# A two-block transformer kernel: filter loads and products of the start, the turning of attention probabilities, gate row, tokens and tail

## Chip, cores and metric

The kernel runs on one core of one Trainium2 chip. Everything is float32. The metric is the device time of one execution in microseconds (us), the median of several runs.

## What is computed

One token sequence of 256 x 1024 goes through two blocks. Cut to what matters:

```python
# first block: modulation from c, then attention and a gated feed-forward network
mod = silu(c) @ w_ada + b_ada                      # 1024 -> 6 x 1024
hn = rms_norm(h, norm1_g) * (1 + scale1) + shift1
qa, ka, va, qb, kb, vb = split(hn @ w_in)          # 1024 -> 3072
o_a = dilated_window_attention(...)                # 8 heads, three windows merged: counts * exp(s)
p = softmax(q1 k1 + bias) - lam * softmax(q2 k2 + bias); o_b = p @ v   # 4 heads
h = h + gate1 * ([o_a, o_b] @ w_out)
h = h + gate2 * ((silu(gate) * val) @ w_down)      # 1024 -> 5632, conv, 2816 -> 1024
# second block: long convolution (Hyena) beside a gated linear recurrence, then experts
z = sin(fr1 * (pos @ w1 + b1)); z = sin(fr2 * (z @ w2 + b2)); filt = (z @ w3) * window
aff = softmax(h @ router_w); gates, idx = top_k(aff.T, 32)   # 16 experts take 32 tokens each
y = (silu(xg @ w1[e]) * (xg @ w3[e])) @ w2[e] * gates        # 1024 -> 2048 -> 1024 per expert
return rmsnorm(x + g2 * scatter(y), final_g)
```

## The kernel before

It is one program with five instruction streams written out by hand, one per engine, that wait for each other on semaphores. `S["name"]` is a semaphore; `done(ins, name)` raises it on VectorE, and `link` makes VectorE wait for its own instruction. The order on an engine is the order in its function. `MM` is a TensorE product; one float32 product is two MATMUL records in the profile, a transpose is one.

Weights come in units of 1 MB, issued by SyncE in the order of `units` into `ring`, which has 8 slots; a slot is refilled when the unit in it is used (`unit_done`). The first eight units are the first third of the modulation weights w_ada. `mod_products(m)` multiplies unit m with the conditioning, in four column groups; `copy_mod_rows(g)` on ScalarE copies the rows of eight such units out, and `mod_columns(g)` turns them with four transposes. `third_layer` multiplies the filter's hidden values (`sint`) with `w3w`, one product for each of eight pieces. VectorE's `window` reads them. `features` are the products of the input projection with `w_in`, a unit of 32 records each. Counts for the windows (`cntW`) come over GpSimd's queue.

The attention goes in 16 pairs p. Pairs 0 to 7 are two heads of the first kind and a block of 128 queries; pairs 8 to 15 (`isb`) are the two maps of one head of the second kind. TensorE's loop over p is: `scores(p + 2)`, a modulation product (p < 6), `turn_probs(p)`, a modulation product (6 <= p < 14), `pv(p - 1)`. VectorE does `pair_max(p)` (bias and maximum, into `sS`), the sum and reciprocal and `diag` (`pair_diag(p)`: the identity scaled by 1/sum), and `pair_out(p)`. ScalarE does the exponentials of p (into `sE`) and then the copy of the turned probabilities of p - 1 (`probs_copied`). `turn_probs` multiplies the probabilities with `diag`, which turns and scales them at once:

```python
if isb:
    last = MM(PTB[...], sE[:, b, i, ...], diag[:, b, i, :], start=(i == 0), stop=(i == 1))
else:
    last = MM(PTB[...], sC[:, b, i, ...], diag[:, b, i, :], start=True, stop=True)
```

In the routing VectorE ranks 16 x 256 affinities in four rounds of `max` and `match_replace`, TensorE meanwhile turns the tokens (`token_major`), and broadcasts the gate row (`gate_rows`), and then it turns the places. An expert then goes through `expert_pick` (32 tokens, products with a one-hot `ohx`), a copy on ScalarE (`xrow`), two transposes (`tokens_turned`), `expert_tokens` on VectorE (gain, then shift, into `xe`), `expert_up` (16 units), `expert_gate_rows`, `expert_down` (8 units) and `expert_scatter`. Expert weights come in pairs of units, 2 MB each, 12 pairs an expert, 192 in all, into eleven places in SBUF (`PAIR`). Pair g is issued when pair g - 11 is used (`expert_unit_done`), so pair 11 waits for the first two units of the first expert. The last pair comes as two units. At the end ScalarE squares the four banks of 128x512, VectorE makes the inverse and multiplies (`final_rows`), and SyncE stores two blocks of 512 KB.

## Time and profile before

| | |
|---|---|
| median of 3 runs | 1646.39 us (1646.09 to 1648.83) |
| the profiled execution | 1647.9 us, its span 1646.1 us |
| TensorE busy | 77% of the span, weight loads 43% |
| VectorE, ScalarE, GpSimd busy | 24%, 13%, 3% |
| chain that ended last | TensorE 48%, DMA 42%, VectorE 4% |
| mean granted TensorE clock | 0.895 |

The span is the time from the first to the last instruction of the profiled execution; its own time is 1.8 us longer. The median of the runs is 1.5 us below that time. PE is TensorE, DVE is VectorE, ACT is ScalarE, POOL is GpSimd, SP is SyncE; PEld are weight loads.

### The profile page before, as it was taken

How to read it: one execution, taken by the hardware profiler on the slowest of the kernel's cores; microseconds unless marked ns; L12 is line 12 of the kernel's file. 1: busy time of each engine (PE TensorE's matmuls, PEld its weight loads, DVE VectorE, ACT ScalarE, POOL GpSimd, SP SyncE). 2: the span in 40 equal slices, each digit the busy share in tenths (PEclk: the TensorE clock that was granted, in tenths of full speed). 3: DMA queues.
4: the chain of work that ended last, by engine and by line, in shares of the span. 5: the costliest groups of instructions: out<-in, count | busy, mean ns of one | idle time of the engine just before them, and what ended most of it. 6: DMA issues, size and time to landing. Idle time of an engine off the chain costs nothing.

```text
span 1646.1 us, 16563 instructions
## 1 busy us (share of the span) xinstructions
PE 1272.1 (77%) x7160; PEld 702.0 (43%) x7160; DVE 394.1 (24%) x800; ACT 217.3 (13%) x423; POOL 51.0 (3%) x75
## 2 busy tenths in 40 slices
PE   5999999999999999988555655665665656666555
PEld 3776678888888878852111111111111111111111
DVE  4577653454032547530000000000000000000001
ACT  2323422122202231120000000000000000000001
...
GB/s 359 205 195 287 322 191 325 214 228 214 199 154 136 176 127 178 205 262 425 428 427 428 428 428 427 427 428 428 428 427 428 428 428 429 427 427 429 428 428 286
DMA packets 109978, 545.04 MB, mean 331 GB/s; under 512 B 5908, under 2 KB 73269, under 8 KB 78997
## 3 DMA queue, kind: packets, MB, share of 16 engines
...
## 4 chain that ended last, share of the span: by engine, by line
PE 48%; DMA 42%; DVE 4%; another core or an unknown queue 3%; ACT 1%; issue 1%; SPq 0%; DVEq 0%
DMA arena<-in_exp_w_dram 29%; PE L L1594 12%; DMA ring<-in_exp_w_dram 9%; PE L L1821 7%; PE X L2029 5%; PE L L1790 4%; DMA tok<-in_exp_w_dram 3%; PE X L1762 3%; PE X L2057 2%; PE L L1940 2%; PE L L1728 2%; DMA ring<-in_w_ada_dram 2%; PE L L2068 1%; PE L L1605 1%; PE X L1870 1%
## 5 line engine op out<-in xcount | busy, mean ns | idle before, releaser
L2029 PE MATMUL X<-arena,HR 128*32 128x512 f32 x1104 | 171.1, 753 | 102.9 <-DMA arena<-in_exp_w_dram 93.0
L1594 PE MATMUL L<-tok,ring 128*128 128x256 f32 x960 | 213.0, 383 | 2.0 <-ACT tok L605 1.6
L1594 PEld LDWEIGHTS L<-tok,ring 128*128 128x128 f32 x960 | 183.7, 192 | 34.8 <-issue 9.8
L2029 PE MATMUL X<-ring,HR 128*32 128x512 f32 x784 | 119.1, 736 | 82.5 <-DMA ring<-in_exp_w_dram 77.5
L2057 PE MATMUL X<-arena,HI 128*32 128x512 f32 x592 | 94.9, 772 | 56.7 <-DMA arena<-in_exp_w_dram 52.6
L1436 DVE TENSOR_TENSOR HR<-HR,X 128x512 f32<-128x512 f32 x16 | 11.0, 688 | 515.6 <-ACT HR L860 515.6
L2029 PEld LDWEIGHTS X<-arena,HR 128*32 128x32 f32 x1104 | 34.3, 125 | 230.0 <-DMA arena<-in_exp_w_dram 153.3
L1821 PE MATMUL L<-tok,ring 128*128 128x256 f32 x448 | 99.4, 379 | 0.0
L2029 PEld LDWEIGHTS X<-ring,HR 128*32 128x32 f32 x784 | 23.6, 120 | 168.8 <-DMA ring<-in_exp_w_dram 120.7
L1821 PEld LDWEIGHTS L<-tok,ring 128*128 128x128 f32 x448 | 84.3, 190 | 13.5 <-issue 2.8
L2057 PE MATMUL X<-ring,HI 128*32 128x512 f32 x320 | 55.3, 826 | 32.8 <-DMA ring<-in_exp_w_dram 30.1
L860 ACT ACTIVATE HR<-X 128x512 f32<-128x512 f32 x16 | 9.6, 597 | 528.1 <-PE X L2029 528.1
L1790 PE MATMUL L<-arena,ring 128*128 128x256 f32 x352 | 77.5, 379 | 0.3 <-DVE arena L1196 0.3
L1441 DVE TENSOR_TENSOR HI<-X,HI 128x512 f32<-128x512 f32 x16 | 11.1, 692 | 277.5 <-PE X L2057 277.5
L1790 PEld LDWEIGHTS L<-arena,ring 128*128 128x128 f32 x352 | 66.7, 190 | 9.7 <-DVE arena L1196 0.7
L2057 PEld LDWEIGHTS X<-arena,HI 128*32 128x32 f32 x592 | 18.7, 127 | 122.2 <-DMA arena<-in_exp_w_dram 82.0
L2068 PE MATMUL L<-HI,HR 64*128 64x512 f32 x128 | 38.9, 730 | 14.5 <-DVE HI L1441 14.5
L858 ACT ACTIVATE HR<-X 128x256 f32<-128x256 f32 x16 | 6.1, 384 | 312.0 <-PE X L2012 312.0
L2029 PE MATMUL X<-tok,HR 128*32 128x512 f32 x160 | 27.8, 831 | 18.4 <-DMA tok<-in_exp_w_dram 17.3
L2057 PEld LDWEIGHTS X<-ring,HI 128*32 128x32 f32 x320 | 10.2, 132 | 72.4 <-DMA ring<-in_exp_w_dram 49.3
L1190 DVE SCALAR_TENSOR_TENSOR arena<-L,cols,arena 128x255 f32<-128x255 f32 x44 | 19.2, 478 | 79.8 <-ACT arena L724 79.8
L549 POOL TENSOR_TENSOR HI<-HI 128x256 f32<-128x256 f32 x16 | 9.9, 617 | 883.4 <-DVE HI L1446 820.5
...
## 6 DMA issues: line engine op xcount, KB each, us to landing
...
ring<-in_w_in_dram SPq DMA_DIRECT2D x34, 1024.0 KB, 5.5
...
ring<-in_w_ada_dram SPq DMA_DIRECT2D x24, 1024.0 KB, 8.8
ring<-in_w_up_dram SPq DMA_DIRECT2D x22, 1024.0 KB, 7.3
arena<-in_ada_w_dram POOLq DMA_DIRECT2D x13, 1024.0 KB, 7.2
ring<-in_ada_w_dram SPq DMA_DIRECT2D x11, 1024.0 KB, 5.0
```

Source lines behind the costliest of these rows:

```text
L1190: last = V.scalar_tensor_tensor(o_[:, 1:T], u_[:, 0:T - 1], colC[:, C_W0 + c:C_W0 + c + 1], o_[:, 1:T], ALU.mult, ALU.add)
L1594: last = MM(L[:, j % 4, m * T:m * T + T], w[:, k, m * P:m * P + P], src(k), start=(k == 0), stop=(k == KT - 1))
L1605: last = MM(L[:, j % 4, t * T:t * T + T], src[:, k, t * P:t * P + P], w[:, k, :], start=(k == 0), stop=(k == KT - 1))
L1728: last = MM(L[:, j % 4, m * T:m * T + T], w[:, k, m * P:m * P + P], oT[:, k, :], start=(k == 0 and m == 0), stop=(k == KT - 1), skip_group ...
L1762: last = MM(bank[:, x * T:x * T + T], wk, hk, start=(k == 0), stop=(k == KT - 1))
L1790: last = MM(L[:, pos["wdn"][m // 2] % 4, (m % 2) * T:(m % 2) * T + T], w[:, kk, m * P:m * P + P], aT[:, 2 * i + kk, :], start=(i == 0 and ...
L1821: last = MM(L[:, j % 4, x * T:x * T + T], wk, hk, start=(k == 0), stop=(k == KT - 1))
L1870: last = MM(o_, uA[(n - 1) % 2][:, h, t * P:t * P + P], crossed(h, t, LEVELS[n - 1]), start=True, stop=True)
L1940: last = MM(L[:, j % 4, m * T:m * T + T], w[:, k, m * P:m * P + P], yTh[:, k, :] if k < HG else yTg[:, k - HG, :], start=(k == 0 and m == ...
L2029: last = MM(X[CAP * j:CAP * j + CAP, w, :], xe[:, k % 2, k // 2, :], mslot(g, u)[:, j * 512:j * 512 + 512], start=(k == 0), stop=(k == KT ...
L2057: last = MM(X[CAP * b:CAP * b + CAP, 2, :], hTe[:, 2 * x + c, CAP * j:CAP * j + CAP], mslot(g, u)[:, c * D + nb * 512:c * D + nb * 512 + 5 ...
L2068: MM(XB[2 * n + t], ge[h0:h0 + HD, t, :], ys[h0:h0 + HD, :], start=False, stop=True, skip_group_check=True).then_inc(S["scatter_done"], 1)
```

## The change

Its name says: mixer order; filter loads in 128 rows with products dealt, and scaled probabilities; gate row and tokens in parts, with turned identities. What it does:

- The three small inputs of the sine layers become one array of 128 x 448, the third filter matrix one of 128 x 1024 (two halves of its columns below each other) in place of 64 x 2048. Both, and the window, are loaded over ScalarE's queue, with the identity first. The counts are loaded later, behind the last unit of the first eight. The second sine layer is computed twice, on partitions 0 to 63 and 64 to 127.
- The four first filter products stand between `mod_products` 4, 5, 6 and 7 (one, two, one). `keep_busy(bank, n)` puts n transposes of the identity, which nobody reads, into a bank: 3 and 8 around `mod_columns(0)`, 4, 7, 2 and 3 in the routing and the first expert, 13, 2 and 4 in the last expert.
- The probabilities are scaled by ScalarE (`probs_scaled`) and then turned by plain transposes. For the second kind of head VectorE first combines the two maps. ScalarE's copy of the turned ones comes one pair later than before.
- The gate row is computed in two halves, after the first and the third ranking round; its copy comes behind the four token copies; the places go to another bank. The token copies go by blocks of tokens. `expert_tokens` works on two halves.
- The last unit lands in two halves; the final squares take two banks at once; the output is stored in four parts of 256 KB.

```diff
+def filter_rows(v, z):
+
+    w1, w2, w3 = (np.asarray(v[f"hy_pos_w{n}_2"], np.float32)[0] for n in (1, 2, 3))
+    sine = np.zeros((P, T + 192), np.float32)
+    sine[0:33, 0:T], sine[0:33, T:T + 64] = z, w1
+    sine[0:64, T + 64:T + 192] = np.concatenate([w2, w2], axis=1)
+    return sine, w3.reshape(64, 2, 2 * C).transpose(1, 0, 2).reshape(P, 2, C)
...
+        zw, w1w, w2w = sinew[0:33, 0:T], sinew[0:33, T:T + 64], sinew[0:64, T + 64:T + 192]
...
-                if n == 2:
-                    sp.dma_start(w3w[0:64, :], a["hy_pos_w3_2"][0]).then_inc(S["filter_landed"], 16)
-                    sp.dma_start(winw[:, :, :], a["k_win"]).then_inc(S["filter_landed"], 16)
...
-                sp.dma_start(mslot(g, 1), w[e, j, :, 2048:4096]).then_inc(S["last_unit_landed"], 16)
+                for c in range(2):
+                    sp.dma_start(mslot(g, 1)[:, c * D:c * D + D], w[e, j, :, 2048 + c * D:2048 + c * D + D]).then_inc(S[f"last_half{c}_landed"], 16)
...
-                sp.wait_ge(S["out_ready"], t + 1)
-                sp.dma_start(out[0, t * P:t * P + P, :], outw[:, t, :]).then_inc(S["out_stored"], 16)
-            sp.wait_ge(S["out_stored"], 16 * TT)
+                for n in range(2):
+                    sp.wait_ge(S["out_ready"], 2 * t + n + 1)
+                    sp.dma_start(out[0, t * P:t * P + P, n * 512:n * 512 + 512], outw[:, t, n * 512:n * 512 + 512]).then_inc(S["out_stored"], 16)
+            sp.wait_ge(S["out_stored"], 32 * TT)
...
             load(dftE[:, :, :, :], a["k_dft"][:, 0:2, :, :], "dftE_landed")
+            load(cntW[:, :], a["k_cnt"], "counts_landed")
...
+            load(sq0[:, :], a["k_sq0"], "sq0_landed")
             load(cols[:, :], a["p_cols"], "cols_landed")
-            load(sq0[:, :], a["k_sq0"], "sq0_landed")
-            for dst, src in ((zw[0:33, :], a["k_z"]), (w1w[0:33, :], a["hy_pos_w1_2"][0]), (w2w[0:64, :], a["hy_pos_w2_2"][0])):
-                load(dst, src, "sine_landed")
+            load(sinew[:, :], a["p_sine"], "sine_landed")
+            load(w3w[:, :, :], a["p_third"], "filter_landed")
+            load(winw[:, :, :], a["k_win"], "filter_landed")
...
-                        act.wait_ge(S["probs_turned"], p - 1)
+                        act.wait_ge(S["inv_ready"], p - 1)
...
+                if 1 <= p <= NP_:
+                    q = p - 1
+                    b = q % 2
+                    act.wait_ge(S["inv_ready"], q + 1)
+                    for i in range(2 if q < 8 else 1):
+                        last = A(sC[:, b, i, :], sC[:, b, i, :], ACT.Copy, scale=rz[:, 2 * b + i:2 * b + i + 1])
+                    last.then_inc(S["probs_scaled"], 1)
                 if p in (6, 15):
                     copy_mod_rows(1 if p == 6 else 2)
-                if p >= 1:
-                    q = p - 1
+                if p >= 2:
+                    q = p - 2
...
-                A(x2[:, n % 2, (n // 2) * 512:(n // 2) * 512 + 512], XB[n], ACT.Copy, scale=rr[:, n % 2:n % 2 + 1]).then_inc(S["lin_emptied_by_act"], 1)
+                A(x2[:, n // 2, (n % 2) * 512:(n % 2) * 512 + 512], XB[n], ACT.Copy, scale=rr[:, n // 2:n // 2 + 1]).then_inc(S["lin_emptied_by_act"], 1)
+            act.wait_ge(S["gate_rows"], 1)
+            A(g2b[:, :], X[:, 2, :], ACT.Copy).then_inc(S["gate_row_ready"], 1)
...
+                act.wait_ge(S["scatter_done"], 4 * NE - 2 + 2 * t)
+                b0 = pos["xnat"][2 * t] % 4
+                A(outw[:, t, :].rearrange("p (n d) -> p n d", n=2), L[:, b0:b0 + 2, :], ACT.Square,
+                  accum_out=fs[:, t:t + 1]).then_inc(S["final_sq"], 1)
...
-                link(V.reciprocal(rz[:, 2 * b:2 * b + 2], zs[:, 2 * b:2 * b + 2]))
+                inv = V.reciprocal(rz[:, 2 * b:2 * b + 2], zs[:, 2 * b:2 * b + 2])
                 if isb:
-                    link(V.tensor_scalar(rz[:, 2 * b + 1:2 * b + 2], rz[:, 2 * b + 1:2 * b + 2], neglam, None, ALU.mult))
-                for i in range(2):
-                    last = V.tensor_scalar(diag[:, b, i, :], ident, rz[:, 2 * b + i:2 * b + i + 1], None, ALU.mult)
-                done(last, "diag_ready")
+                    link(inv)
+                    r1 = rz[:, 2 * b + 1:2 * b + 2]
+                    link(V.scalar_tensor_tensor(r1, r1, neglam, zs[:, 2 * b:2 * b + 1], ALU.mult, ALU.mult))
+                    inv = V.scalar_tensor_tensor(sC[:, b, 0, :], sE[:, b, 1, :], r1, sE[:, b, 0, :], ALU.mult, ALU.add)
+                done(inv, "inv_ready")
...
+                turned = TURNB.rearrange("p (x q c) -> p x q c", x=2, q=4)
+                for x in range(2):
+                    V.tensor_tensor(xe[:, x, :, :], turned[:, x, :, :], gain_of[:, x, :, :], ALU.mult).then_inc(S["expert_scaled"], 1)
+                    dve.wait_ge(S["expert_scaled"], 2 * e + x + 1)
+                    V.tensor_tensor(xe[:, x, :, :], xe[:, x, :, :], shift_of[:, x, :, :], ALU.add).then_inc(S["expert_tokens"], 1)
...
+            def keep_busy(bank, n):
+
+                for _ in range(n):
+                    nc.tensor.transpose(bank[:, 0:P], ident, ident)
...
-            for m in range(1, 4):
+            MM(aux("sin2")[:, 0:T], w2w, sint[0:64, 1, :], start=True, stop=True).then_inc(S["sin2_done"], 1)
+            for m in range(1, 8):
                 mod_products(m)
-            third_layer(0)
-            for m in range(4, 8):
-                mod_products(m)
+                if 4 <= m < 7:
+                    third_layer((0, 1, 3)[m - 4], (1, 2, 1)[m - 4])
+            keep_busy(X[:, 2, :], 3)
             mod_columns(0)
+            keep_busy(X[:, 2, :], 8)
...
-                pe.wait_ge(S["diag_ready"], p + 1)
+                pe.wait_ge(S["probs_scaled"], p + 1)
                 if p >= 1:
                     pe.wait_ge(S["probs_copied"], p)
-                for kt in range(TT):
-                    for i in range(2):
-                        if isb:
-                            last = MM(PTB[:, kt * P:kt * P + P], sE[:, b, i, kt * P:kt * P + P], diag[:, b, i, :], start=(i == 0), stop=(i == 1))
-                        else:
-                            last = MM(PTB[:, (2 * i + kt) * P:(2 * i + kt) * P + P], sC[:, b, i, kt * P:kt * P + P], diag[:, b, i, :], start=True, stop=True)
+                for i in range(1 if isb else 2):
+                    for kt in range(TT):
+                        last = nc.tensor.transpose(PTB[:, (2 * i + kt) * P:(2 * i + kt) * P + P], sC[:, b, i, kt * P:kt * P + P], ident)
                 last.then_inc(S["probs_turned"], 1)
...
-            for k in range(KT):
-                h0 = HD * (k // 4)
-                last = MM(X[h0:h0 + HD, 2, (k % 4) * P:(k % 4) * P + P], ones[:, 0:HD], dg[:, k, :], start=True, stop=True)
+            for part in range(2):
+                pe.wait_ge(S["ranked"], 1 + 2 * part)
+                for k in range(4 * part, 4 * part + 4):
+                    h0 = HD * (k // 4)
+                    last = MM(X[h0:h0 + HD, 2, (k % 4) * P:(k % 4) * P + P], ones[:, 0:HD], dg[:, k, :], start=True, stop=True)
+                keep_busy(X[:, 0, :], (4, 7)[part])
             last.then_inc(S["gate_rows"], 1)
-            pe.wait_ge(S["gate_row_ready"], 1)
             reached(pe, "places")
             for t in range(TT):
-                last = nc.tensor.transpose(X[:, 2, t * NE:t * NE + NE], rs[0:NE, 2, t * P:t * P + P], ident[0:NE, 0:NE])
+                last = nc.tensor.transpose(X[:, 1, t * NE:t * NE + NE], rs[0:NE, 2, t * P:t * P + P], ident[0:NE, 0:NE])
...
+                if e == 0:
+                    keep_busy(X[:, 0, :], 2)
...
+                    if u < 2:
+                        pe.wait_ge(S["expert_tokens"], 2 * e + u + 1)
...
-                    elif g == LASTG:
-                        pe.wait_ge(S["last_unit_landed"], 16)
                     j, x = (u - 16) // 2, (u - 16) % 2
                     for c in range(2):
+                        if g == LASTG and x == 1:
+                            pe.wait_ge(S[f"last_half{c}_landed"], 16)
...
+                    if e == NE - 1:
+                        keep_busy(X[:, 0, :], {19: 13, 21: 2, 23: 4}.get(u, 0))
```

How this stands in the streams: first TensorE at the start. L1540 is `mod_products` (4 products a unit), L1570 `third_layer`, L1561 `mod_columns`, L1594 the first projection unit. Before:

```order
L1616 MATMUL L<-arena 64x256
L1540 MATMUL X<-ring,HI 32x512 x12
L1570 MATMUL L<-arena 128x512 x4
L1540 MATMUL X<-ring,HI 32x512 x16
L1561 MATMUL X<-sq,HI 128x128 x4
L1594 MATMUL L<-tok,ring 128x256 x16
```

And in the change, where L1567 is `mod_products`, L1598 `third_layer`, L1516 `keep_busy`, L1588 `mod_columns` and L1622 the projection:

```order
L1644 MATMUL L<-arena 128x256
L1567 MATMUL X<-ring,HI 32x512 x16
L1598 MATMUL L<-arena 128x512
L1567 MATMUL X<-ring,HI 32x512 x4
L1598 MATMUL L<-arena 128x512 x2
L1567 MATMUL X<-ring,HI 32x512 x4
L1598 MATMUL L<-arena 128x512
L1567 MATMUL X<-ring,HI 32x512 x4
L1516 MATMUL X<-sq 128x128 x3
L1588 MATMUL X<-sq,HI 128x128 x4
L1516 MATMUL X<-sq 128x128 x8
L1622 MATMUL L<-tok,ring 128x256 x16
```

The filter products no longer stand together ahead of four units, but one, two and one between them.

Second, ScalarE in the attention, at the pairs where the first kind of head begins. L685 are exponentials, L695 the copy of turned probabilities. Before:

```order
L685 ACTIVATE arena<-arena,small 128x256 x4
L695 ACTIVATE arena<-L 128x512
L685 ACTIVATE arena<-arena,small 128x256 x2
L695 ACTIVATE arena<-L 128x512
L685 ACTIVATE arena<-arena,small 128x256 x2
```

And in the change, where L698 are exponentials, L705 the scalings and L715 the copy:

```order
L698 ACTIVATE arena<-arena,small 128x256 x4
L705 ACTIVATE arena<-arena,small 128x256 x2
L698 ACTIVATE arena<-arena,small 128x256 x2
L705 ACTIVATE arena<-arena,small 128x256 x2
L715 ACTIVATE arena<-L 128x512
L698 ACTIVATE arena<-arena,small 128x256 x2
L705 ACTIVATE arena<-arena,small 128x256 x2
L715 ACTIVATE arena<-L 128x512
```

The first copy stands behind the exponentials of two more pairs and the scalings of one more pair.

Third, TensorE in the routing. L1974 is `token_major`, L2000 the gate row, L2005 the places, L2012 the first pick, L2017 its transposes and L2029 the first expert's products. Before:

```order
L1974 MATMUL L<-sq,tok 128x128 x4
L2000 MATMUL X<-HI,sq 64x128 x8
L2005 MATMUL X<-sq,rs 128x16 x2
L2012 MATMUL X<-tok,HI 32x256 x8
L2017 MATMUL X<-sq,HR 128x128 x2
L2029 MATMUL X<-arena,HR 32x512 x16
```

And in the change, with L2028 the gate row and L1516 `keep_busy`:

```order
L2000 MATMUL L<-sq,tok 128x128 x4
L2028 MATMUL X<-HI,sq 64x128 x4
L1516 MATMUL X<-sq 128x128 x4
L2028 MATMUL X<-HI,sq 64x128 x4
L1516 MATMUL X<-sq 128x128 x7
L2033 MATMUL X<-sq,rs 128x16 x2
L2040 MATMUL X<-tok,HI 32x256 x8
L1516 MATMUL X<-sq 128x128 x2
L2047 MATMUL X<-sq,HR 128x128 x2
L1516 MATMUL X<-sq 128x128 x3
L2062 MATMUL X<-arena,HR 32x512 x16
```

Eleven transposes now stand between the gate row and the places, and five around the turning of the first tokens.

## Rows read from the trace of the kernel before

**Rows 1.** The page, part 2: GB/s in 40 equal slices of the span.

```profile
GB/s 359 205 195 287 322 191 325 214 228 214 199 154 136 176 127 178 205 262 425 428 427 428 428 428 427 427 428 428 428 427 428 428 428 429 427 427 429 428 428 286
```

**Rows 2.** Timeline, TensorE at the start: start us, us, what, records, idle before.

```profile
33.48 1.46 PE L1540 MATMUL X<-ring,HI 128*32 128x512 f32 x8 [2.32 <-DMA ring<-in_w_ada_dram]
35.64 1.12 PE L1561 MATMUL X<-sq,HI 128*128 128x128 f32 x4 [0.70 <-ACT HI L593]
38.38 10.05 PE L1594 MATMUL L<-tok,ring 128*128 128x256 f32 x32 [1.62 <-ACT tok L605]
...
52.95 7.17 PE L1594 MATMUL L<-tok,ring 128*128 128x256 f32 x32
```

**Rows 3.** Windows: busy by engine, then granted clock, DMA share and GB/s.

```profile
16.00:18.00 2.00, 2.00 (x11) 1.77 (x10) 1.86 (x8) 0.04 (x1) 0.00 (x0) 1.00 0.95 201
...
36.00:37.00 1.00, 0.76 (x4) 0.35 (x2) 0.17 (x1) 0.00 (x0) 0.00 (x0) 0.50 1.11 350
```

**Rows 4.** SyncE's issues from 19.75 us, and the first one's time to landing.

```profile
19.75 34.91 SPq L437 DMA_DIRECT2D ring<-in_w_in_dram  x9
...
ring<-in_w_in_dram SPq DMA_DIRECT2D x1, 1024.0 KB, 16.7
```

**Rows 5.** Timeline: TensorE's transposes, at the kernel's start and at 93 us.

```profile
10.08 3.64 PE L1497 MATMUL L<-sq,arena 128*128 128x128 f32 x16 [10.08 <-DMA sq<-in_k_sq_dram]
...
14.97 3.72 PE L1515 MATMUL X<-tok,sq 128*128 128x256 f32 x16
...
93.24 1.91 PE L1497 MATMUL L<-sq,arena 128*128 128x128 f32 x16
```

**Rows 6.** Timeline, TensorE in the attention: a round of each half.

```profile
165.29 1.06 PE L1540 MATMUL L<-ring,arena 128*32 128x512 f32 x8
...
166.29 1.16 PE L1669 MATMUL L<-arena 128*128 128x128 f32 x8
...
167.38 0.67 PE L1683 MATMUL L<-arena 128*64 128x128 f32 x8
...
167.97 0.70 PE L1656 MATMUL X<-arena 64*128 64x256 f32 x4
...
168.60 1.06 PE L1540 MATMUL L<-ring,arena 128*32 128x512 f32 x8
...
189.10 1.16 PE L1667 MATMUL L<-arena 128*128 128x128 f32 x8
...
192.46 1.16 PE L1667 MATMUL L<-arena 128*128 128x128 f32 x8
```

**Rows 7.** Groups by form from 157 to 206 us: count, busy us, mean ns.

```profile
L1057 DVE CUSTOM_DVE_ANT_0 arena<-X,arena 128x256 f32<-128x256 f32 x28 | 10.8, 422 | 12.7 <-PE X L1656 12.7
...
L682 ACT ACTIVATE arena<-arena,small 128x256 f32<-128x256 f32 x16 | 7.9, 497 | 0.0
...
L695 ACT ACTIVATE arena<-L 128x256 f32<-128x256 f32 x8 | 3.1, 384 | 14.3 <-PE L L1667 14.3
```

**Rows 8.** Timeline, routing: places, pick, first expert's products, SyncE's issue of pair 11.

```profile
730.28 0.31 PE L2005 MATMUL X<-sq,rs 16*128 16x16 f32 x2 [3.07 <-DVE rs L1417]
...
730.90 1.93 PE L2012 MATMUL X<-tok,HI 128*32 128x256 f32 x16 [0.32 <-DVE HI L1420]
...
735.01 5.35 PE L2029 MATMUL X<-arena,HR 128*32 128x512 f32 x24 [0.97 <-DVE HR L1428]
...
738.72 0.33 SPq L453 DMA_DIRECT2D arena<-in_exp_w_dram  x1
```

**Rows 9.** Windows there, columns as in rows 3.

```profile
734.00:735.00 1.00, 0.04 (x1) 0.00 (x0) 0.85 (x2) 0.59 (x1) 0.00 (x0) 0.50 0.47 197
...
736.00:737.00 1.00, 1.00 (x12) 0.26 (x8) 0.00 (x0) 0.00 (x0) 0.00 (x0) 0.50 0.00 0
```

**Rows 10.** Timeline, tail: the last unit's products, the last rows multiplied.

```profile
1634.22 1.06 PE L2057 MATMUL X<-arena,HI 128*32 128x512 f32 x8 [1.42 <-DMA arena<-in_exp_w_dram]
...
1641.64 1.41 DVE L1472 SCALAR_TENSOR_TENSOR tok<-L,HI,ring 128x512 f32<-128x512 f32 x2 [0.27 <-ACT HI L875]
```

86 lines of the change are left out of this document (40 added, 46 removed).

## The prediction

> **What bounds the kernel now.** I read the page first. In its GB/s line [rows 1] the last 22 of 40 slices stand at 427 or 428 (the very last lower): from about 740 us to 1634 us the experts' weights stream in without a hole, one pair of units (2 MB) every 4.9 us, and TensorE waits for them. Nothing that shortens work inside this stream is worth anything there. Everything ahead of it is worth its full length, because the stream can only fill its eleven buffers early; after that it needs TensorE to free them. So I read the timeline and the windows of the start, of the attention and of the routing, and last the timeline of the tail.
>
> At the start TensorE waits for the last unit of the first modulation (2.32 us idle ahead of 33.48), and from there the granted clock is 0.50, the lower level of 1.2 GHz: the first unit of the input projection takes 10.05 us, a later one 7.17 [rows 2, 3]. From there to 675 us TensorE is nearly always busy, so what is won early is passed on. In the attention one round takes 3.31 us in the first half and 3.36 in the second, and TensorE goes through its four steps without a wait [rows 6]. In the routing TensorE stands idle for 3.07 us, the clock falls to 0.50, and the first experts' products run at half speed; the DMA engines are empty meanwhile, since buffer 0 is freed only after two units [rows 8, 9].
>
> **Start.** (a) The third filter matrix (512 KB) went to 64 partitions. The two microseconds in which it arrives carry 201 GB/s at a busy share of 0.95 [rows 3], where the stream has 428. That is 0.45 MB lost, 1.1 us at 428; with a little of it in the neighbouring window I take 1.2 us, bounds 0 and 1.5. The sine inputs grow by about 0.17 MB and the counts (0.19 MB) are moved behind the last unit, which cancel. All of it stands ahead of the last modulation unit, so that one lands at 32.2 instead of 33.4. The first w_in unit landed at 36.4 (issued at 19.75, 16.7 us [rows 4]); it comes earlier too, at 35.2. (b) The four filter products are dealt between the units, so that TensorE's longest idle ahead of the last unit is about 1.2 us, and three and eight transposes fill the waits around the turning of the modulation. If the clock stays at 2.4 GHz: 2.9 us on the first projection unit (10.05 less 7.17), 0.4 on the last modulation unit (1.46 [rows 2] against 1.06 at the upper level [rows 6]), 0.5 on its four transposes (1.12 [rows 2] against 4 x 0.12, from 16 in 1.91 [rows 5], and their start-up). That is 3.8. The projection could then start at 36.2, a microsecond behind its landed unit, so DMA doesn't take it back. Start: 5.0 us, bounds 0 and 5.5. The two fills cost nothing: ScalarE's copy and VectorE's scaling hide them (TensorE waits 0.70 and 1.62 us there [rows 2], the fills take 0.36 and 0.96).
>
> **Attention.** Removed on TensorE: eight passes per round (1.09 us [rows 6]) become four transposes (0.50) in the first half and two (0.3) in the second. TensorE alone would then need 2.7 and 2.5 us per round. On VectorE two scalings go, and in the second half a combination of 128x256 (0.42, as its maxima [rows 7]) comes. ScalarE gets two scalings of 128x256 per round or one (0.38 each, as its copy of that size [rows 7]). What decides is the path from one round's scores to those two rounds later: scores 0.75, two maxima and a negation 0.95, exponentials 1.1 (two of 0.50 [rows 7] with their sums), scaling 0.45, copy 0.4, transposes 0.3, then modulation product 1.0 and value product 0.64 in front of the next scores: 5.6 for two rounds, 2.8 each, and 2.9 with the hops. The copy of round p now stands on ScalarE behind the exponentials of p+2 and the scaling of p+1, and the transposes of p+1 wait for it. So: five rounds of the first half gain 0.5 (2.5); six of the second gain 0.45 (2.7); ahead of the first transposes the scaling adds 0.45; the copy of the modulation rows, which waits for a product of the same round, stalls one round (0.7); the last rounds, which have no product to hide behind, gain nothing. Sum 4.0. Lower bound 0 (each hop 0.4 longer), upper bound 9 (TensorE alone: 7 x 0.6 + 6 x 0.85). I take 4.0, nearer the path than TensorE's own time. The modulation units don't bind: 1 MB per 2.9 us is 360 GB/s against 428.
>
> **Routing and first expert.** Removed: into the idle 3.07 us goes the later half of the gate row's products (under 1 us) and eleven transposes (1.3 us at 0.12), in two groups; they fit, so they delay nothing. Until 730.90 nothing moves. Then, at 2.4 GHz, the pick takes half of 1.93 and a little, its transposes 0.2 less; the tokens come in two parts of 128x128, the first after about 0.5 us instead of 0.9 (two operations, 0.42 each for 128x256 as in [rows 7]); and the two units that free buffer 0 take 1.8 instead of 3.7 us (735.01 to 738.72). Sum 0.9 + 0.2 + 0.4 + 1.9 = 3.4: the issue at 738.72 comes 3.4 us earlier. The DMA engines ran empty in the microsecond from 734 on and moved 0 GB/s at 736 [rows 9], so all of it is won: 3.4, bounds 0.4 (the clock stays low) and 4.2 (the whole hole). From the second expert on the clock and the split tokens lie under the stream: nothing. Moving the gate row's copy behind the token copies, and the places into another bank, costs nothing, since expert 0 needs it only behind its sixteen units of products.
>
> **Tail.** The last unit lands in halves, so 0.43 us of its 1.06 [rows 10] runs ahead; one add (0.2) goes; the squares of a row block are one operation of 128x1024 instead of two of 512 (0.1 each); the last store is 256 KB instead of 512, issued after the second of the two row products [rows 10], and with fewer bytes behind it: 0.6 us. The clock was already up here, so the 19 fills gain nothing. Sum 1.4, bounds 0.6 and 2.
>
> **Sum.** 5.0 + 4.0 + 3.4 + 1.4 = 13.8 us. The profiled execution took 1647.9 us (span 1646.1 and 1.8 around it), so it would take 1634.1; the median of the runs, 1646.39, becomes 1632.6. Nothing between the parts takes it back: from 207 to 675 us the work is the same and TensorE-bound, and DMA has slack.
>
> **A rule against it.** The first 16 transposes of the kernel, with nothing else on TensorE, take 3.64 us, the same 16 later 1.91, and the products right behind the first ones (14.97) run at 3.72 us for 16, 0.23 each, the upper level [rows 5]. So here the clock rose on transposes alone (the clock column misses it; the durations show it). The Trainium skill (TensorE: Matmul & The Clock Gate, Part 4: PE-mode transpose) says that the full clock doesn't engage for transposes, as they don't count as busy in the same way. By that rule no fill would hold the clock: start 1.2, routing 0.5, and the sum would be 7.1 instead of 13.8. The trace speaks against the rule for the rise; for holding, nothing in it decides.
>
> **Rivals.**
> 1. The fills don't hold the clock at one or both places. For it: 3 transposes in 0.35 us of a 0.6 us wait leave holes, and only a rise on transposes was seen. Against: the fall came each time after an idle of over 2 us, and no such idle is left. One place lost: gain 10 to 11, 1636; both: 7, 1639.5. Chance 0.17.
> 2. The attention gains nothing, since ScalarE's hop gives back what TensorE saves (each round's path 0.4 us longer than summed). For it: the last rounds have no slack. Gain 10, 1636.5. Chance 0.08.
> 3. The change doesn't do what it says or the holes return later: a queue behind the expert stream's first issues, or the start hidden behind w_in's landing. Gain under 3.3, 1645. Chance 0.04. What is called mixer order appears nowhere as an order of the units; it is the order of the token copies, worth nothing.
> 4. Slower: with transposes not counted, the attention's thinner mix of products (2.7 of work in a 2.9 us round, 0.5 of it transposes) lets the clock fall there. Its 2.7 and 2.5 us become 5.0 and 4.2, rounds 1.7 and 0.8 above today's: 20 us lost against 10 won elsewhere, 1656. It decides from a round of 4.0 us on (3.3 + 10/16). Against: three quarters of the round are ordinary products. Chance 0.03.
>
> **How the numbers follow.** Forecast 0.68: 1632.6, its own range 1629.5 to 1635.5 from the bounds of attention and start. Rivals 1 and 2 (0.25) reach 1639.5; I take the range to 1638, which holds 1 in one place and 2, and from 1629. Within 0.2% (3.3 us, about what a measurement of this kernel can tell) is rival 3 with the edge of both clocks lost: 0.05. Faster by more 0.91, slower by more 0.04.
>
> **What would show it.** Start: granted clock 1.00 from 30 to 45 us, first projection unit at about 36 us and 7.2 us long; if 10 us long, rival 1. Attention: transposes every 2.8 to 2.9 us, four steps with waits for ScalarE's copy; at 3.3, rival 2; products at half speed, rival 4. Routing: clock 1.00 at 731, the first issue after the eleventh pair 5.0 us after the places' transposes (8.4 before), the hole in GB/s about 1 us. Tail: 10.5 us from the last landing to the end instead of 11.9. The prediction would be wrong most if a clock falls or if the stream's 4.89 us per pair itself changes: 0.02 us there are 3.6 us.

## The result and the profile after

| | before | after |
|---|---|---|
| median | 1646.91 us (4 runs, 1646.09 to 1648.83) | 1631.97 us (4 runs, 1631.30 to 1632.51) |
| profiled execution, its span | 1647.9, 1646.1 us | 1632.01, 1630.2 us |
| mean granted TensorE clock | 0.895 | 0.905 |

The ratio is 0.9907, with a 95% interval of 0.989 to 0.9925. By the medians 14.9 us are gone, by the two profiled executions 15.9. The forecast was a gain of 13.8 and a time of 1632.6 us. The kernel before has a median of 1646.91 here, since a fourth run has joined the three of 1646.39.

The page's GB/s line of after, beside [rows 1]. The stream is as full as before (427 to 429), and the slice in which it begins stands at 320 instead of 262:

```profile
GB/s 373 218 231 291 316 231 285 232 232 210 176 155 166 144 132 197 184 320 429 427 427 429 428 427 429 428 427 427 428 429 427 427 428 429 427 427 427 429 428 298
```

TensorE at the start of after (timeline: start us, us, what, records, idle before), beside [rows 2]. L1542 is `sum_squares`, L1567 `mod_products`, L1588 `mod_columns`, L1516 `keep_busy`, L1622 the projection, L1598 `third_layer`:

```profile
14.45 5.84 PE L1542 MATMUL X<-tok,sq 128*128 128x256 f32 x16
...
31.20 1.06 PE L1567 MATMUL X<-ring,HI 128*32 128x512 f32 x8
...
32.98 0.66 PE L1588 MATMUL X<-sq,HI 128*128 128x128 f32 x4 [0.24 <-ACT HI L606]
33.48 1.04 PE L1516 MATMUL X<-sq 128*128 128x128 f32 x8
35.26 7.14 PE L1622 MATMUL L<-tok,ring 128*128 128x256 f32 x32 [0.75 <-ACT tok L618]
42.33 2.38 PE L1598 MATMUL L<-arena 64*128 64x512 f32 x8
...
45.59 7.17 PE L1622 MATMUL L<-tok,ring 128*128 128x256 f32 x32
```

Windows of after (us, busy of each engine with its records, then granted clock, DMA share, GB/s), beside [rows 3, 9]:

```profile
16.00:18.00 2.00, 2.00 (x6) 1.58 (x5) 1.61 (x9) 0.54 (x2) 0.00 (x0) 1.00 1.01 416
36.00:37.00 1.00, 1.00 (x6) 0.90 (x5) 1.00 (x4) 1.00 (x3) 0.00 (x0) 1.00 1.01 373
723.00:724.00 1.00, 1.00 (x16) 0.38 (x12) 0.00 (x0) 0.00 (x0) 0.00 (x0) 1.00 0.12 49
724.00:725.00 1.00, 1.00 (x16) 0.28 (x11) 0.00 (x0) 0.00 (x0) 0.00 (x0) 1.00 0.12 33
```

The last modulation unit starts at 31.20 instead of 33.48 and takes 1.06 us instead of 1.46. The first projection unit starts at 35.26 instead of 38.38 and takes 7.14 instead of 10.05, at a granted clock of 1.00 where it was 0.50. The second one starts at 45.59 instead of 52.95: the start won 7.4 us, and 1.33 of them lie where the prediction had nothing. From the first to the second projection unit it is 10.33 us (45.59 less 35.26), before 14.57 [rows 2]; 2.91 of the difference is the clock of the first unit, the rest the four filter products between them (2.38 us). The window at 16 us carries 416 GB/s instead of 201; that at 723 carries 49, the one behind it 33: the hole of the DMA engines in the routing is shorter, not closed.

TensorE in the attention of after, beside [rows 6]. L1695 are the transposes of the probabilities, L1705 and L1709 the value products, L1685 the scores, L1754 the output projection:

```profile
157.99 0.66 PE L1695 MATMUL L<-sq,arena 128*128 128x128 f32 x4
158.58 0.67 PE L1709 MATMUL L<-arena 128*64 128x128 f32 x8
159.17 0.70 PE L1685 MATMUL X<-arena 64*128 64x256 f32 x4
159.81 1.06 PE L1567 MATMUL L<-ring,arena 128*32 128x512 f32 x8
160.80 0.66 PE L1695 MATMUL L<-sq,arena 128*128 128x128 f32 x4
...
164.98 0.63 PE L1695 MATMUL L<-sq,arena 128*128 128x128 f32 x4 [1.30 <-ACT arena L715]
...
191.53 0.41 PE L1695 MATMUL L<-sq,arena 128*128 128x128 f32 x2 [1.46 <-ACT arena L715]
...
195.32 3.69 PE L1754 MATMUL L<-arena,ring 128*128 128x256 f32 x16 [0.62 <-DVE arena L1104]
```

A round of the first half takes 2.81 us (157.99 to 160.80) where it took 3.31, and its four steps follow each other without a wait. Two waits for ScalarE's copy (L715) stand out, 1.30 us at 164.98 and 1.46 at 191.53. From the first scores to the first output projection it is 195.32 less 143.57, 51.75 us, before 206.78 less 150.93, 55.85: 4.1 won. In the kernel before, the transposes of pair 14 (which start at 191.53 in after) and the output projection:

```profile
201.81 1.06 PE L1667 MATMUL L<-arena 128*128 128x128 f32 x8
...
206.78 3.69 PE L1728 MATMUL L<-arena,ring 128*128 128x256 f32 x16 [0.62 <-DVE arena L1083]
```

Routing, SyncE's issue of pair 11 and tail of after, beside [rows 8, 10]:

```profile
718.75 0.29 PE L2033 MATMUL X<-sq,rs 16*128 16x16 f32 x2 [0.44 <-DVE rs L1439]
719.36 1.07 PE L2040 MATMUL X<-tok,HI 128*32 128x256 f32 x16 [0.31 <-DVE HI L1442]
...
722.14 3.64 PE L2062 MATMUL X<-arena,HR 128*32 128x512 f32 x32 [0.38 <-DVE HR L1452]
...
724.13 2.04 SPq L463 DMA_DIRECT2D arena<-in_exp_w_dram  x2
...
1618.15 1.05 PE L2090 MATMUL X<-arena,HI 128*32 128x512 f32 x4 [0.21 <-DMA arena<-in_exp_w_dram]
1619.40 1.05 PE L2090 MATMUL X<-arena,HI 128*32 128x512 f32 x4 [0.20 <-DMA arena<-in_exp_w_dram]
...
1626.30 1.41 DVE L1495 SCALAR_TENSOR_TENSOR tok<-L,HI,ring 128x512 f32<-128x512 f32 x2 [0.27 <-ACT HI L894]
```

The issue comes 5.38 us after the places' transposes (718.75 to 724.13); before it was 8.44. From the last landing (1619.40) to the end of the span (1630.2) it is 10.8 us, before 11.9.

### The profile page after: what moved, and what is told of

It reads as the page before. It is cut to its first block, busy times and chain, and to the rows that moved or that the text cites. A ratio compares the mean times of both kernels' runs of the same rounds, so it can differ in the third digit from the quotient of the medians.

```text
span 1630.2 us, 16551 instructions
## 1 busy us (share of the span) xinstructions
PE 1258.2 (77%) x7126; PEld 692.9 (43%) x7126; DVE 393.2 (24%) x806; ACT 227.5 (14%) x443; POOL 50.8 (3%) x75
## 4 chain that ended last, share of the span: by engine, by line
PE 47%; DMA 44%; DVE 5%; ACT 2%; issue 1%; SPq 0%; another core or an unknown queue 0%; ACTq 0%; DVEq 0%
DMA arena<-in_exp_w_dram 26%; DMA ring<-in_exp_w_dram 15%; PE L L1622 12%; PE L L1847 7%; PE L L1816 5%; DMA tok<-in_exp_w_dram 3%; PE X L2090 3%; PE X L2062 3%; PE X L1788 3%; PE L L2103 2%; PE L L1966 2%; PE L L1754 2%; PE X L2040 1%; PE L L1633 1%; PE X L1896 1%
## 5 line engine op out<-in xcount | busy, mean ns | idle before, releaser
L2062 PE MATMUL X<-arena,HR 128*32 128x512 f32 x1104 | 164.1, 725 | 97.2 <-DMA arena<-in_exp_w_dram 90.4
L1622 PE MATMUL L<-tok,ring 128*128 128x256 f32 x960 | 210.1, 380 | 1.2 <-ACT tok L618 0.7
L2062 PE MATMUL X<-ring,HR 128*32 128x512 f32 x784 | 128.6, 788 | 87.7 <-DMA ring<-in_exp_w_dram 84.1
L1622 PEld LDWEIGHTS L<-tok,ring 128*128 128x128 f32 x960 | 181.6, 190 | 32.9 <-issue 8.8
L2090 PE MATMUL X<-arena,HI 128*32 128x512 f32 x592 | 99.9, 799 | 61.7 <-DMA arena<-in_exp_w_dram 58.8
L2090 PE MATMUL X<-ring,HI 128*32 128x512 f32 x320 | 47.0, 714 | 31.3 <-DMA ring<-in_exp_w_dram 27.9
L2103 PE MATMUL L<-HI,HR 64*128 64x512 f32 x128 | 35.4, 672 | 13.9 <-DVE HI L1465 13.9
```

What stands on the lines that cost most here:

```text
L1622: last = MM(L[:, j % 4, m * T:m * T + T], w[:, k, m * P:m * P + P], src(k), start=(k == 0), stop=(k == KT - 1))
L2062: last = MM(X[CAP * j:CAP * j + CAP, w, :], xe[:, k % 2, k // 2, :], mslot(g, u)[:, j * 512:j * 512 + 512], start=(k == 0), stop=(k == KT ...
L2090: last = MM(X[CAP * b:CAP * b + CAP, 2, :], hTe[:, 2 * x + c, CAP * j:CAP * j + CAP], mslot(g, u)[:, c * D + nb * 512:c * D + nb * 512 + 5 ...
L2103: MM(XB[2 * t + n], ge[h0:h0 + HD, t, :], ys[h0:h0 + HD, :], start=False, stop=True, skip_group_check=True).then_inc(S["scatter_done"], 1)
```

## Experiments

All are edits of the changed kernel; their times stand beside its median of 1631.97 us. They ran in three groups, each beside the kernel before, whose medians there were 1646.59, 1647.70 and 1647.90 us. So a difference of under a microsecond between a median and that of the change says little, and the traces decide it. The 95% interval of each ratio to before reaches about 2.5 us to either side and overlaps that of the change in every experiment. Single runs separate better: where an experiment came out slower, all its runs lie above the four of the change, except without the start's transposes, with alternating products and with whole tokens, where they overlap.

### What held the clock at the start: no transposes

```diff
-            keep_busy(X[:, 2, :], 3)
             mod_columns(0)
-            keep_busy(X[:, 2, :], 8)
```

> The changed kernel without the three and the eight transposes of the identity around the turning of the first modulation; the dealt filter products, the loads and all else stay. Theory (the transposes hold the granted clock at 1.00): as in the kernel before, TensorE waits for ScalarE's and VectorE's steps with nothing to do, the clock falls to 0.50 by the first projection unit, which takes about 10 us instead of 7.14; the four turned columns take about 1.1 us instead of 0.66; time 2.5 to 3.5 us above the change, about 1635. Rival (what kept the clock is that no wait ahead of the last modulation unit is longer than about a microsecond, since the filter products are dealt between the units and that unit lands earlier): the clock stays at 1.00 without the transposes, the first projection unit takes 7.1 us, and the time is that of the change, 1632 within 0.5.

Measured: 1633.08 us, with runs from 1631.53 to 1634.71, a wider spread than the 1.2 us of the change. The profile is the one of 1634.71 us. TensorE in it, then windows as above:

```profile
32.92 0.66 PE L1588 MATMUL X<-sq,HI 128*128 128x128 f32 x4 [0.72 <-ACT HI L606]
35.20 7.14 PE L1622 MATMUL L<-tok,ring 128*128 128x256 f32 x32 [1.62 <-ACT tok L618]
...
195.84 5.82 PE L1752 MATMUL L<-arena,ring 128*128 128x256 f32 x16 [0.62 <-DVE arena L1104]
```

```profile
36.00:37.00 1.00, 1.00 (x7) 0.87 (x6) 1.00 (x4) 1.00 (x4) 0.00 (x0) 1.00 1.06 401
193.00:195.00 2.00, 2.00 (x12) 1.93 (x11) 0.29 (x1) 0.27 (x1) 0.00 (x0) 0.58 1.04 410
195.00:200.00 5.00, 4.38 (x12) 3.38 (x11) 4.20 (x4) 2.43 (x3) 0.00 (x0) 0.50 0.75 313
```

The rival won in the trace, though the median lies 1.1 us above the change and not within the 0.5 it gave. Without a transpose the clock is 1.00 at 36 us, the projection starts at 35.20 (35.26 with them) and takes the same 7.14 us, though TensorE stands idle for 1.62 us right ahead of it. So the theory fell for the start: without the eleven transposes there nothing gets longer. What this run lost it lost elsewhere. At 193 us, behind the wait at the end of the attention, its clock fell to 0.50, and the first sixteen records of the output projection took 5.82 us where after has 3.69. From 193 to 199 us it lost 2.7 us against after. This lies far from the edit and comes back below in runs with other edits.

### No idle transposes at all, and none in the routing

The second kernel drops every `keep_busy`, the other the four calls in the routing and the first expert:

```diff
-                keep_busy(X[:, 0, :], (4, 7)[part])
...
-                if e == 0:
-                    keep_busy(X[:, 0, :], 2)
...
-                if e == 0:
-                    keep_busy(X[:, 0, :], 3)
```

> The changed kernel without any transpose of the identity: neither at the start nor in the routing, the first expert and the last expert. Theory (they hold the clock at both places): start as in the run before, 2.5 to 3.5 us; and in the routing the pick takes 1.9 us instead of 1.07, the first two units of expert products 3.7 us instead of 1.84, so the issue of the twelfth pair comes 2.5 to 3 us later; together 5 to 6.5 us above the change, about 1637.5. The tail is the same length, since its clock was at 1.00 before too: 10.8 us from the last landing to the end. Rival (no fill matters, the dealt work alone keeps the clock): 1632. Rival of the tail: the 19 fills there hold something, tail over 11.3 us.

> The changed kernel without the sixteen idle transposes in the routing and the first expert; those of the start and the tail stay. Theory (they and nothing else hold the clock there): as in the run without any, the granted clock falls to 0.50 about 2 us after the places' transposes, the first 32 product records take 5.9 us instead of 3.64, the issue of pair 11 comes 7.3 us after the places' transposes instead of 5.38, time 1.8 to 2.2 us above the change, 1634. Rival (the fall of that one run was chance): below 1632.7, clock 1.00 in the profile.

Measured: 1634.90 us without any (1633.41 to 1635.91), 2.9 above the change where 5 to 6.5 were expected, and 1633.68 without those of the routing (1633.06 to 1636.39). TensorE, SyncE's issue and two windows of the latter:

```profile
36.14 7.14 PE L1622 MATMUL L<-tok,ring 128*128 128x256 f32 x32 [0.75 <-ACT tok L618]
...
719.61 0.29 PE L2032 MATMUL X<-sq,rs 16*128 16x16 f32 x2 [1.35 <-DVE rs L1439]
720.22 1.58 PE L2039 MATMUL X<-tok,HI 128*32 128x256 f32 x16 [0.31 <-DVE HI L1442]
...
723.69 5.49 PE L2057 MATMUL X<-arena,HR 128*32 128x512 f32 x32 [0.71 <-DVE HR L1452]
...
727.39 2.18 SPq L463 DMA_DIRECT2D arena<-in_exp_w_dram  x2
```

```profile
722.00:723.00 1.00, 0.70 (x2) 0.32 (x2) 0.00 (x0) 0.98 (x2) 0.00 (x0) 0.50 1.15 492
725.00:726.00 1.00, 1.00 (x8) 0.19 (x4) 0.00 (x0) 0.00 (x0) 0.00 (x0) 0.50 0.00 0
```

Here the theory held: the clock falls to 0.50 in the pick, the 32 records take 5.49 us instead of 3.64, and the issue comes 7.78 us after the places' transposes instead of 5.38. In the profile of the kernel without any it was 7.35 (719.51 to 726.86), with the clock at 0.50 from 721 to 727 us. So the sixteen transposes are worth 2.0 to 2.4 us in the profiles and 1.7 in the median. All sixteen were taken away together; which of them hold the clock, the eleven ahead of the places or the five behind the pick, is open. With no fill at the start the first projection unit again took 7.14 us at a granted clock of 1.00, the second such profile. Without the 19 in the tail it is 10.8 us from the last landing to the end (1621.93 to 1632.7), the length of after: nothing there gets longer without them. The median without any is 1.2 us above that without those of the routing, and in its group the gain on before is 11.7 us against 14.2. No trace shows what of the start or the tail would make up that difference, and it stays open.

Both profiles also show something that no edit made. The last modulation unit landed about 0.8 to 0.9 us later than in after, and the first projection unit started at 36.04 and 36.14 instead of 35.26; in the profile with whole tokens it was 36.20. In the other runs with the start's loads unchanged it starts between 34.87 and 35.39. So the start alone moves by up to 1.3 us between executions, and why the landing moves isn't shown.

### The third filter matrix in 64 rows

```diff
-    return sine, w3.reshape(64, 2, 2 * C).transpose(1, 0, 2).reshape(P, 2, C)
+    return sine, w3
...
-            load(w3w[:, :, :], a["p_third"], "filter_landed")
+            load(w3w[0:64, :], a["p_third"], "filter_landed")
...
-                    MM(aux("w3", n), parity(sint[h0:h0 + 64, 3, :], t), w3w[h0:h0 + 64, q % 2, :], start=True, stop=True)
+                    MM(aux("w3", n), parity(sint[0:64, 3, :], t), w3w[0:64, q * C:q * C + C], start=True, stop=True)
```

> The changed kernel with the third filter matrix as 64 x 2048 on partitions 0 to 63, loaded at the same place of the same queue, and all eight filter products on those partitions. Theory (the slow load of 64 rows and the products on one half of the rows were what the start lost): the last modulation unit's products start 1.1 to 1.5 us later than 31.20, the second four filter products take 3.7 us instead of 2.38, and the second projection unit starts about 2.5 us later than 45.59; time 2.0 to 2.8 us above the change, 1634 to 1635. Rival (the landing came earlier through the new order of the small loads, not through the rows): the last modulation unit starts within 0.4 us of 31.20, and only the 1.3 us of the products is lost, 1633.3.

Measured: 1634.92 us (1634.21 to 1635.40), 2.95 above. TensorE, GpSimd's issue and windows (L1597 is `third_layer` here):

```profile
29.10 1.99 PE L1597 MATMUL L<-arena 64*128 64x512 f32 x4
...
33.20 1.06 PE L1567 MATMUL X<-ring,HI 128*32 128x512 f32 x8
33.44 0.76 POOL L505 DMA_DIRECT2D arena<-in_ctx_dram  x1 [28.53 <-DMA ring<-in_w_ada_dram]
...
44.33 3.71 PE L1597 MATMUL L<-arena 64*128 64x512 f32 x8
...
48.92 7.17 PE L1621 MATMUL L<-tok,ring 128*128 128x256 f32 x32
```

```profile
12.00:14.00 2.00, 0.52 (x2) 0.28 (x2) 0.83 (x2) 1.49 (x3) 0.00 (x0) 0.87 1.10 267
14.00:16.00 2.00, 2.00 (x6) 1.21 (x5) 1.27 (x4) 0.00 (x0) 0.00 (x0) 0.50 0.97 221
16.00:18.00 2.00, 2.00 (x6) 1.64 (x5) 1.68 (x9) 0.47 (x2) 0.00 (x0) 0.50 0.96 373
```

The theory held, and its numbers were low. While 64 rows are filled, the four microseconds from 12 carry 267 and 221 GB/s and the next two 373, where after has 420, 422 and 416. GpSimd's next load, which waits for the landing of the last modulation unit, is issued at 33.44 instead of 31.44, and that unit's products start 2.0 us later. The four filter products behind the first projection unit take 3.71 us instead of 2.38, and two of the dealt ones (29.10) 1.99 instead of 1.14. The second projection unit starts 3.3 us later. One profile stands behind the 2.0 us: in the other runs of the changed start GpSimd's load is issued between 31.05 and 32.38, so the landing is 1.1 to 2.4 us later than theirs. And the run shows one thing more: the unit's products start at 33.20, nearly as late as in the kernel before (33.48), but with the dealt products TensorE never waits over 0.25 us from 25.61 until then, and the clock stays at 1.00.

### Filter products in turn on the two halves

```diff
-    return sine, w3.reshape(64, 2, 2 * C).transpose(1, 0, 2).reshape(P, 2, C)
+    return sine, w3.reshape(64, 2, 2, C).transpose(2, 0, 1, 3).reshape(P, 2, C)
...
-                    h0 = 64 * (q // 2)
+                    h0 = 64 * (q % 2)
...
-                    MM(..., w3w[h0:h0 + 64, q % 2, :], start=True, stop=True)
+                    MM(..., w3w[h0:h0 + 64, q // 2, :], start=True, stop=True)
```

> The changed kernel with the columns of the third filter matrix dealt to the two halves of the partitions in turn, so that adjacent filter products alternate between partitions 0 to 63 and 64 to 127 (0, 64, 0, 64 instead of 0, 0, 64, 64). In the changed kernel the batch of four behind the first projection unit takes 2.38 us instead of 3.71, though only one pair of neighbours lies on different halves. Theory (products on different halves of the rows run at the same time): two pairs overlap now, the batch takes 1.7 to 2.1 us, and the second projection unit starts 0.3 to 0.7 us earlier behind the first than the 10.33 us of the change; time 0.3 to 0.7 us lower. Rival (the order of the four doesn't matter, the batch is limited by something else such as its start): 2.38 us again, no change.

Measured: 1634.10 us; three runs at 1634.10 to 1634.35 and two at 1631.86 and 1631.92. TensorE and a window:

```profile
42.13 2.37 PE L1598 MATMUL L<-arena 64*128 64x512 f32 x8
```

```profile
193.00:195.00 2.00, 2.00 (x12) 2.00 (x10) 0.29 (x1) 0.12 (x1) 0.00 (x0) 0.50 0.99 389
```

The theory fell: the four products take 2.37 us in this order and 2.38 in the other. That the use of both halves shortens them is shown by the run with 64 rows; how they overlap inside the four is not. The profile is one of the slower three, and its loss is again the clock at the end of the attention: 0.50 at 193 us, and again 2.7 us lost against after from there to 199 us.

### The attention as before

The edit puts back `pair_diag`, the products with `diag` in `turn_probs`, and ScalarE's copy one pair after the exponentials, as the diff above shows them removed.

> The changed kernel with the attention of the kernel before: probabilities turned and scaled by a product with the diagonal of VectorE, ScalarE's copy one pair after the exponentials. Theory (scaled probabilities and plain transposes gain what the two traces differ by, 4.1 us between the first scores and the first output projection): rounds of 3.3 us again, time 3.5 to 4.5 us above the change, about 1636. Rival (part of the difference is the earlier arrival of the modulation units or a shift of the waits that later stages give back): less than 2.5 us.

Measured: 1635.54 us (1635.43 to 1636.88), 3.6 above. From the first scores (143.18) to the first output projection (199.04) it is 55.86 us, as long as in the kernel before, against 51.75 in after. The theory held.

### Modulation rows behind the copy

```diff
-                if p in (6, 15):
-                    copy_mod_rows(1 if p == 6 else 2)
                 if p >= 2:
...
                     A(pT[...], PTB[:, 0:n * P], ACT.Copy).then_inc(S["probs_copied"], 1)
+                if p in (6, 15):
+                    copy_mod_rows(1 if p == 6 else 2)
```

> The changed kernel, but on ScalarE the copies of the modulation rows (at pairs 6 and 15) stand behind the copy of the turned probabilities of the same round instead of ahead of it. In the changed kernel TensorE waits 1.30 us for that copy at 164.98 and 1.46 us at 191.53. Theory (the order on ScalarE is what is left of the stalls): each of the two waits becomes at most 0.7 us, the first output projection starts 1.0 to 1.6 us earlier than 195.32, and the time falls by as much, to about 1630.7; the shorter waits also make the drop of the clock rarer that the run without the start's transposes showed at 193 us. Rival (the waits only move: the next pair's copy is late by the same 0.6 us, since VectorE's maxima and the exponentials set the round): less than 0.4 us.

Measured: 1630.80 us (1629.94 to 1631.42), 1.2 below. TensorE:

```profile
166.69 0.63 PE L1695 MATMUL L<-sq,arena 128*128 128x128 f32 x4 [1.06 <-ACT arena L713]
...
190.51 0.41 PE L1695 MATMUL L<-sq,arena 128*128 128x128 f32 x2 [0.97 <-ACT arena L713]
...
194.30 3.69 PE L1754 MATMUL L<-arena,ring 128*128 128x256 f32 x16 [0.62 <-DVE arena L1104]
```

The waits become 1.06 and 0.97 us, above the 0.7 expected, and the output projection starts 1.02 us earlier. So the order of two copies on ScalarE made up 1.0 to 1.2 us of the stalls; the larger part of the 1.30 and 1.46 us is still there.

### Pair 11 in halves

```diff
+                if g == NPAIR:
+                    sp.dma_start(mslot(g, 0), w[e, j, :, 0:2048]).then_inc(S["first_refill"], 16)
+                    sp.wait_ge(S["expert_unit_done"], 2)
+                    sp.dma_start(mslot(g, 1), w[e, j, :, 2048:4096]).then_inc(S[f"pair{g % NPAIR}_landed"], 16)
+                    return
...
-                sp.wait_ge(S["expert_unit_done"], 2 * (g - NPAIR + 1))
+                sp.wait_ge(S["expert_unit_done"], 1 if g == NPAIR else 2 * (g - NPAIR + 1))
```

> The changed kernel with pair 11 (the first one that waits for a buffer of the expert stream to come free) issued as two units, each as soon as its half of buffer 0 has been used. Theory (the DMA engines stand empty from about 723 to 725 us, so each microsecond of an earlier issue is won for the whole stream): the first issue comes 0.9 us earlier, 4.5 us after the turned places instead of 5.38, the windows at 723 to 725 carry more, and the time falls by 0.8 to 0.9 us, to 1631.1. Rival (a transfer of 1 MB alone starts no earlier, or the second half's wait costs the queue as much): no change within 0.3 us.

Measured: 1630.96 us (1630.61 to 1631.18), 1.0 below. SyncE's issues, then a window:

```profile
723.35 0.33 SPq L465 DMA_DIRECT2D arena<-in_exp_w_dram  x1
724.21 0.33 SPq L467 DMA_DIRECT2D arena<-in_exp_w_dram  x1
```

```profile
724.00:725.00 1.00, 1.00 (x16) 0.36 (x12) 0.00 (x0) 0.00 (x0) 0.00 (x0) 1.00 0.80 139
```

The places' transposes start at 718.83 here, so the first issue comes after 4.52 us, and 724 to 725 us carries 139 GB/s instead of 33. The 0.86 us by which it is issued earlier come back in the time.

### The tail as before

The edit puts back the last unit in one transfer, the four squares with their add, and two stores of 512 KB.

> The changed kernel with the tail of the kernel before: the last unit in one transfer, four squares of 128x512 with an add, two stores of 512 KB; the idle transposes stay. Theory (the tail gained 1.1 us: 0.55 behind the last row product through the smaller store, the rest through squares and the add, nothing through the halves of the last unit, whose second four records take 1.05 us like eight): 11.9 us again from the last landing to the end, time 0.9 to 1.3 us above the change, 1633. Rival (the halves gained their 0.43 us too): 1.4 us or more above.

Measured: 1632.99 us (1632.71 to 1634.12), 1.0 above. The last unit's products and the last rows:

```profile
1619.32 1.07 PE L2090 MATMUL X<-arena,HI 128*32 128x512 f32 x8 [1.42 <-DMA arena<-in_exp_w_dram]
...
1626.74 1.41 DVE L1494 SCALAR_TENSOR_TENSOR tok<-L,HI,ring 128x512 f32<-128x512 f32 x2 [0.27 <-ACT HI L892]
```

The whole unit takes 1.07 us; in after each half of it takes 1.05 (1618.15 and 1619.40), and the second starts no earlier than the whole one. So the halves win nothing: four records take as long as eight. In the kernel each half's products go to only two of the four column groups, which would explain it, but no run tests another split. From the last landing to the start of the last row products it is 7.42 us here and 6.90 in after (squares and add, 0.5); from there to the end of the span 4.46 and 3.90 (the smaller store, 0.56).

### Transposes at the end of the attention

```diff
+                if p == 14:
+                    pe.wait_ge(S["max_ready"], 15)
+                    keep_busy(X[:, 0, :], 8)
                 if p < 16:
                     turn_probs(p)
...
+            keep_busy(X[:, 0, :], 4)
             pe.wait_ge(S["probs_copied"], 16)
```

> The changed kernel with eight idle transposes ahead of the turning of pair 14, where TensorE waits 1.46 us, and four behind the last value products. Theory (after that wait the granted clock falls to 0.50 in some executions, as in one run at 193 to 200 us where it cost 2.1 us on the first sixteen products of the output projection): the fall is gone from every run, the highest of the five is within 1.2 us of the lowest, and the median is up to 1 us below the change, 1631 to 1632. Rival (the fall is not from that wait, or transposes don't hold the clock there): the spread and the median stay, runs of 1633 to 1634.7 still come up.

Measured: 1631.55 us, 1631.12 to 1631.86, the narrowest spread among the kernels with five runs. Of the nine profiles that have the changed attention and its full wait at the end, three show the clock down at 193 us: the runs without the start's transposes, with alternating products, and, for a shorter time, with whole tokens. Of the three in which the wait is filled or shortened (this one, the rows behind the copy, all together) none does. That fits the theory, but it is a count of few, and the median's 0.4 us can't be told from nothing.

### Tokens whole

The edit scales and shifts an expert's tokens in one piece of 128x256.

> The changed kernel with the tokens of an expert scaled and shifted in one piece of 128x256 each, not in two halves. Theory (the first products start after the first half): the first expert's products start 0.3 to 0.5 us later behind the turning of the tokens, issue of pair 11 as much later, time 0.3 to 0.5 us above the change. Rival (the longer wait lets the clock fall, since the three transposes behind the turning don't reach far enough): 2 us or more above. Second rival: nothing, within 0.2.

Measured: 1632.39 us (1631.21 to 1634.02), which says nothing alone; its profile, the slowest run, has the late start and the fall of the clock at 193 us, which the edit doesn't touch. In the profile the first products start 1.49 us behind the turning of the tokens (722.88 to 724.37), in after 1.21 (720.93 to 722.14): the halves are worth 0.28 us, below the 0.3 to 0.5 of the theory.

### Together

> The changed kernel with what won in the runs before put together: modulation rows behind the copy, pair 11 in halves, alternating filter products, five idle transposes ahead of the turning of pair 14 and four behind the last value products. Theory (the gains lie at different places of one chain and add): 1.2 and 1.0 us as measured and 0.3 to 0.7 for the products, so 2.4 to 3 us below the change, 1629.2 within 0.5. Rival (they share a wait, the one for the expert stream's first buffers): 1.5 us or less below.

Measured: 1630.00 us (1629.22 to 1630.40), ratio to before 0.9895, 95% interval 0.9879 to 0.9911. That is 2.0 us below the change, though the two intervals overlap, and short of the 2.4 to 3 expected: the alternating products gave nothing, which leaves the 2.2 of the two edits. It is the fastest version of all.

## Why the prediction was right

The forecast of 1632.6 us was 0.6 above the median, in a range of 1629 to 1638. Some of that closeness is luck: the gain was forecast 1.1 us short by the medians and 2.1 short by the profiles, and the new median of before, 0.5 above the one the forecast began from, made up part of the first. Its steps:

- **Start, 5.0 us: too small, 7.4 measured.** Term (a), the earlier landing, was put at 1.2 us, and the unit started 2.28 earlier; the experiment with 64 rows gives 2.0 of it back. The prediction priced only the one window at 201 GB/s [rows 3]; in the run with 64 rows the load depresses six microseconds. Term (b), the clock, came as forecast: 2.91 on the first projection unit, 0.40 on the modulation unit, 0.46 on its transposes. Missing was a term for the filter products on both halves of the rows, 1.33 us behind the first projection unit. The projection started at 35.26 in this profile, not at 36.2; three others of the changed start have 36.04 to 36.20, so of the 7.4 us some 0.9 depend on the execution.
- **The reason given for (b) was half wrong.** It named the dealt products and the transposes together. The transposes are not needed: two profiles without them keep 1.00. What is shown is that their absence changes nothing. The earlier landing isn't needed either: with 64 rows the last unit's products start at 33.20 and the clock stays at 1.00, the transposes being in place. What is left is the dealing of the filter products, by which the wait of 2.32 us [rows 2] is at most 1.29 us in any of these profiles; no run took that alone away.
- **Attention, 4.0 us: right in the sum,** 4.1 in the traces and 3.6 by the run that undoes it, and partly by luck. Rounds came at the forecast 2.8 us, but in the first half not by ScalarE's path, from which it was summed: between 157.99 and 160.80 TensorE has no wait, so its own four steps make the 2.81 us, which the prediction had put at 2.7. It waits for ScalarE's copy in some rounds only from the stall at 164.98 on (0.61 us at 170.50, 0.34 at 179.56, 0.42 at 185.34). The stall by the copy of the modulation rows was forecast once with 0.7; there were two, of 1.30 and 1.46 us, and 1.2 us came back when the copies changed places. The second stall took 1.0 us of the gain. Against it, the last pairs, forecast to gain nothing, gained 1.2: from the transposes of pair 14 to the output projection it is 3.79 us (191.53 to 195.32) instead of 4.97 (201.81 to 206.78).
- **Routing, 3.4 us: near,** 3.06 measured. The pick took 1.07 as forecast; the halves of the tokens gave 0.28 instead of 0.4, and two units 1.99 us from their start to the issue instead of 1.8. The DMA engines' hole, forecast at about 1 us, is about 2 (49 and 33 GB/s from 723 to 725), and the run with pair 11 in halves wins 1.0 us by shortening it.
- **Tail, 1.4 us: 1.1 measured.** The 0.43 for the halves of the last unit was wrong, the rest (squares, add, smaller store) came at 1.08, near the 1.0 of the forecast. The tail's transposes are worth nothing, as forecast.
- **Sum.** 7.4 + 4.1 + 3.1 + 1.1 are 15.7 of the 15.9 between the profiles; 0.2 lie in the stream. The runs that undo one part each (64 rows 2.95, attention 3.6, routing's transposes 1.7, tail 1.0) account for 9.2 of the 14.9 by the medians. No run undoes the clock at the start, which is 3.8 by the traces. The forecast of 13.8 was low by the start. The time came nearer to the median than to the profile (1634.1 forecast, 1632.0 measured), because the profiled execution of before was 1.5 us above its median, that of after 0.04.
- **The rule.** The start doesn't test whether transposes hold the clock, since it stays up without them. The routing does: with sixteen transposes it is 1.00, without them 0.50 in both profiles. The Trainium skill (TensorE: Matmul & The Clock Gate, Part 4: PE-mode transpose) says that the full clock doesn't engage for transposes. The trace disagrees with it in the routing, where the transposes stand among other products.
- **Rivals.** 1 (the fills hold no clock) did not come; for the start its premise, that fills were needed, was wrong. 2 and 3 did not come. 4 (the clock falls in the attention) did not come as priced: the only round over 4.0 us (4.18, from 160.80 to 164.98) is the one with the stall, at a clock of 1.00. But a fall there exists in small: at the end of the attention, behind the wait of 1.46 us, the clock falls in some executions and costs 1.0 to 2.7 us, which neither profile with the old attention shows. The forecast did not have it. That the wait causes it is argued from a count of few profiles.
